# A second scalar for GpSimd's scaling of the attention weights where there is no gate

## The reference

```python
sk = sinks.astype(jnp.float32)[None, :, :, None, None]
m = jnp.maximum(jnp.max(s, axis=-1, keepdims=True), sk)
e = jnp.exp(s - m)
p = e / (jnp.sum(e, axis=-1, keepdims=True) + jnp.exp(sk - m))
```

## Time and profile before

| what | value |
|---|---|
| time, median of 3 runs | 2685.29 us (2681.62 to 2685.42) |
| the profiled execution | 2683.39 us, its span 2681.2 us |
| mean granted TensorE clock | 0.973 |
| PE busy | 2519.5 us (94%) |
| POOL busy | 1772.3 us (66%), 993 instructions |
| DVE busy | 1330.3 us (50%) |
| ACT busy | 715.8 us (27%) |
| swa attention | about 952 to 1032 us |
| na attention | about 1993 to 2094 us |
| ca attention | about 2145 to 2215 us |

### The profile page before, as it was taken

The page is one execution under the profiler, slowest core; times in us unless marked ns, Lnnn a source line. Parts: engine busy times, 40 slices in busy tenths (PEclk is TensorE's granted clock), DMA queues, the critical chain, the costliest instruction groups (busy, mean ns, idle before and its releaser), DMA issues. The chain is left out here.

```text
span 2681.2 us, 36597 instructions
## 1 busy us (share of the span) xinstructions
PE 2519.5 (94%) x11854; PEld 2038.9 (76%) x11854; DVE 1330.3 (50%) x2616; ACT 715.8 (27%) x1504; POOL 1772.3 (66%) x993
## 2 busy tenths in 40 slices
PE   8998889899999979899998999999999899999998
PEld 6786677588888767688886777777877777787877
DVE  6467886443342575411223566664138334751552
ACT  4305785301101263300112222222016232100002
POOL 4465455577777576577775544455779767687884
PEclk9998999999999989999999999999999999999999
DMA  7682001264563202233332311212423214233332
GB/s 262 188 232 72 1 1 39 94 206 153 176 194 94 63 17 91 74 98 94 96 100 71 102 56 57 62 56 66 108 83 71 82 50 123 79 105 91 89 104 75
DMA packets 420545, 259.73 MB, mean 97 GB/s; under 512 B 62844, under 2 KB 411513, under 8 KB 414017
## 3 DMA queue, kind: packets, MB, share of 16 engines
q1 hardware_dynamic: 395024, 199.47, 25.7%
q10 hardware_dynamic: 25393, 58.63, 6.6%
HBM read 253.86 MB, written 8.10 MB: 98 GB/s over the span
## 5 line engine op out<-in xcount | busy, mean ns | idle before, releaser
L677 POOL TENSOR_TENSOR W<-RAW,zeros 128x1024 fp32r<-128x1024 f32 (+2 forms) x349 | 668.2, 1915 | 657.8 <-PE PA L778 312.8
L684 POOL TENSOR_TENSOR W<-RAW,W 128x1024 fp32r<-128x1024 f32 (+2 forms) x355 | 849.1, 2392 | 49.2 <-ACT W L1543 19.4
L775 PE MATMUL PA<-H,W 128*128 128x512 f32 x1288 | 506.0, 393 | 7.7 <-DVEq L2412 2.3
L778 PE MATMUL PA<-H,W 128*128 128x512 f32 x1288 | 503.4, 391 | 0.0
L775 PE MATMUL PA<-A,W 128*128 128x512 f32 x944 | 373.9, 396 | 16.5 <-DVE A L2038 10.7
L778 PE MATMUL PA<-A,W 128*128 128x512 f32 x944 | 371.8, 394 | 0.0
L786 PE MATMUL PA<-H,W 128*128 128x512 f32 x1288 | 318.3, 389 | 0.0
L775 PEld LDWEIGHTS PA<-H,W 128*128 128x128 f32 x1288 | 242.3, 188 | 62.4 <-POOL W L677 7.4
L778 PEld LDWEIGHTS PA<-H,W 128*128 128x128 f32 x1288 | 242.4, 188 | 50.5 <-issue 0.5
L786 PEld LDWEIGHTS PA<-H,W 128*128 128x128 f32 x1288 | 241.7, 188 | 50.3
L786 PE MATMUL PA<-A,W 128*128 128x512 f32 x944 | 236.7, 393 | 0.0
(11 more groups left out here) (375 smaller groups left out, 3929.8 us busy)
## 6 DMA issues: line engine op xcount, KB each, us to landing
AD<-in_ada_w_dram ACTq DMA_DIRECT2D x40, 1024.0 KB, 5.1
RAW<-in_w_in_dram SPq DMA_DIRECT2D x160, 256.0 KB, 3.1
RAW<-in_mlp_w_up_dram SPq DMA_DIRECT2D x128, 256.0 KB, 3.0
RAW<-in_mlp_w_down_dram SPq DMA_DIRECT2D x128, 256.0 KB, 3.0
RAW<-in_w_up_dram SPq DMA_DIRECT2D x88, 256.0 KB, 3.1
RAW<-in_nsa_w_in_dram SPq DMA_DIRECT2D x40, 256.0 KB, 4.1
RAW<-in_w_down_dram SPq DMA_DIRECT2D x16, 384.0 KB, 3.4
RAW<-in_swa_w_in_dram SPq DMA_DIRECT2D x20, 256.0 KB, 3.3
```

Of the source, the lines that this page charges most:

```text
L677: e.tensor_tensor(W[0][:, s, 0:kc], RAW[:, s, 0:kc], zeros[:, 0:1].rearrange("p (a b) -> p a b", b=1).broadcast_to([P, kc, P]), ALU.add).t ...
L684: e.tensor_tensor(W[1][:, s, 0:kc], RAW[:, s, 0:kc], W[0][:, s, 0:kc].bitcast(F32), ALU.subtract).then_inc(w_split, 1)
L775: pe.matmul(PA[s][:, 0:n], W[0][:, s, k], hi, start=(k == 0), stop=False)
L778: mm = pe.matmul(PA[s][:, 0:n], W[0][:, s, k], lo, start=False, stop=False)
```

## The change

Where a unit has no gate, POOL's tensor_scalar gets a second scalar operand, the first column of the tile of ones, and a second multiplication. The product is the same number. L730 runs 112 times: 64 in swa, 32 in na, 16 in ca. No instruction is added, removed or moved, and no wait changes.

```diff
@@ -727,7 +727,7 @@
                 if grp["all"]:
                     pool.tensor_tensor(blocks4(w), blocks4(w), each4(inverse4, grp), ALU.mult).then_inc(sem("scaled"), 1)
                 elif grp["gate"] is None:
-                    pool.tensor_scalar(w, w, inverse, None, ALU.mult).then_inc(sem("scaled"), 1)
+                    pool.tensor_scalar(w, w, inverse, ones[:, 0:1], ALU.mult, ALU.mult).then_inc(sem("scaled"), 1)
                 else:
                     pool.tensor_scalar(w, w, inverse, grp["gate"][b], ALU.mult, ALU.mult).then_inc(sem("scaled"), 1)
```

## The result

The changed kernel takes 2691.8 us (median of 10 runs, 2685.72 to 2693.91), the kernel before 2684.26 us (median of 10, 2680.94 to 2687.55). The ratio is 1.0027, with a 95% interval from 1.0018 to 1.0037: slower by about 0.27%. The prediction was 2691.6 us. The profiled execution's span is 2689.6 us, 8.4 us above that of before.

The account below looks back on a forecast made before the run. It took na's ring through DVE and ACT, 11.97 us per head, as the bound: +7.9 us from blocking by L684, -1.6 at na's end, 0 in swa and ca, +6.3 on 2685.3 gives 2691.6 us; range 2679.5 to 2697.

Parts of the forecast that it names:

- Part 1: POOL's scalings without a gate: they take L732's 773 and 557 ns, some 70 us less of POOL's work.
- Parts 2 and 3: swa and ca: nothing waits for POOL's scaling there, so 0 us, bounds 0.5 us either way in each.
- Part 4: na: POOL's low split L684 starts earlier and blocks DVE's low queries and keys; +7.9 us over six heads.
- the ring: na: the cycle per head through DVE and ACT alone, from key parts to key parts; 11.97 us per head before.
- R: na: start of DVE's reciprocal of unit 4m+1; key parts foreseen done at R + 5.36, before at R + 3.69.
- PE has room, so it only idles longer: na: PE's own work is 11.1 of 13.4 us per head, so it only idles longer, some 2.2 us per head.
- rival (b): na: DVE is not blocked by L684, so the kernel gets faster; -5.1 us, 2680.2 us; chance 0.17.
- Part 5: na's last turn: PE waits for POOL's last scaling, which ends 2.0 us earlier; -1.6 us, bounds 0 and 2.0.
- its own range: Whole kernel, likeliest case: +4 to +8.5 us, from the parts' bounds and half a microsecond at each of six blockings.
- the within part: Whole kernel: chance that the time stays within 0.2%, 5.4 us, of no change; given as 0.15 + 0.14 + 0.08 = 0.37.
- Rival (a): na: PE's clock falls after the longer waits, on top of the blocking; +8.8 us in all, 2694.1 us; chance 0.17.
- Rival (c): L730 keeps its time, or blockings and gains cancel; 0, 2685.3 us, within 2 us; chance 0.15.

Follow-up runs that it names:

- e6_immediate: The change with the number 1.0 as second scalar instead of the column of ones; 2692.06 us, 1.0033 against the kernel before.
- e2_swa_ca_only: The kernel before with the second scalar in swa and ca alone, na left as before; 2686.30 us, 1.0003 against the kernel before.
- e4: The kernel before, one scalar everywhere, with na's low split moved behind the scaling of unit 4m+3; 2684.96 us, 1.0009 against the kernel before.
- e9: The change with na's low and rounded splits moved away from DVE's instructions with two SBUF inputs, placement faults mended; 2683.49 us, 0.9994 against the kernel before.

## Why the prediction was right

**Part 1, POOL's own time.** Right in kind, too high in size. L732's 773 and 557 ns became 823 and 723. The excess is waiting for the port. Of the wide ones a lone one takes 0.77 to 0.78, as the rows above show. Of the 64 narrow ones 43 stood beside no DVE instruction with two SBUF inputs and took 0.56, as L732 does; the other 21 took 1.06 on average. I foresaw 70 us less of POOL's work, the page has 55.4 less. The narrow ones fell short most: 64 x (1062 - 723) ns = 21.7 us instead of 32.3.

**Parts 2 and 3, swa and ca.** Right as far as can be told: -0.17 and +0.24 us, both inside the spread between profiles of one form, and the change in these two stages alone gives 1.0003, with an interval to 1.0012.

**Part 4, the ring.** The mechanism came out row by row: L684 at R + 1.00 (foreseen R + 1.0), the queries blocked and ending 0.55 us after it (0.55), the key parts done at 2019.24, R + 5.38 (R + 5.36), the bias add never at 2.34. By heads, the period against that of before:

| | foreseen | measured |
|---|---|---|
| first blocked head | +1.67 | 12.13 - 10.41 = +1.72 |
| second | +0.42 | 12.76 - 12.11 = +0.65 |
| four more | 4 x 1.45 = +5.8 | 54.28 - 47.76 = +6.5 |

Together +8.9 where +7.9 was foreseen; the mean period is 13.41 us (13.4). What missed is what the heads give back: it was put too high. In the second head the bias add gave back 2.34 - 1.31 = 1.03 us and not 1.25, for a scaling stood beside it (POOL at 2020.14 above); 1.67 - 1.03 = 0.64 is what was measured. In the four others I subtracted 0.22 us for shorter low values each time. But before the change they were longer in every other head only: 0.64 at 2052.19 and 0.65 at 2076.07, and 0.43 at 2040.40 and 0.42 at 2064.28. The row of 2040.40 stood in the earlier trace rows, and I read it as the price without the tail, not as a head of today. So two of the four heads had nothing to give back, and the others grew by 1.45 as foreseen (11.86 to 13.31). In the two that had nothing to give PE has become late besides: from the key parts to the reciprocal of unit 4m+1 they take 8.56 us instead of 8.33. DVE's timeline in one:

```profile
2053.23 0.69 DVE L1985 CUSTOM_DVE_ANT_0 sc<-PS,BIAS 128x512 f32<-128x512 f32 x1 [0.94 <-PE PS L998]
```

PE had started this head after 1.99 us of idle time, and DVE's mask now waits for its scores. "PE has room, so it only idles longer" failed at such places. The idle times themselves are shorter than the "over 2 us" foreseen: 1.77, 1.41, 1.99, 0.84, 1.98 and 1.02 us ahead of the six heads. e6_immediate shows the same two lengths of period, 13.22 and 13.61, at a granted clock of 1.00.

In one head DVE was first after all. DVE and POOL there (timeline, after):

```profile
2054.83 0.69 DVE L1962 TENSOR_TENSOR QS<-QN,QS 64x512 fp32r<-64x512 f32 x1
2055.55 3.49 DVE L1962 TENSOR_TENSOR KK1l<-KN,KK1h 64x512 fp32r<-64x512 f32 x2
...
2054.84 2.95 POOL L684 TENSOR_TENSOR W<-RAW,W 128x1024 fp32r<-128x1024 f32 x1
```

The queries, 0.01 us ahead, keep their 0.69 us; L684 takes 0.55 us longer than its 2.40, gets in between queries and keys, and the first key part takes the 2.8 us instead. That is what was said against rival (b): being second costs the same.

**Part 5, the end.** From the last key parts to the first panel of the projection: 22.3 us before, 20.2 after, -2.1 where -1.6 was foreseen (bounds 0 and 2.0, so a little outside). Part of it may not be the change's. In e2_swa_ca_only, where na is that of before, the same stretch took 21.5 us; against that it is -1.3. As foreseen, POOL's last scaling is no longer waited for, and the next late are ACT's copies and DVE's parts behind them: PE waits 0.84 us for `TURN` of L2010 at 2102.25.

**What was not in the sum.** The first period of na was 9.39 us in the profile of before and 10.4 to 10.6 in every other profile, e2's too. That microsecond belongs to the one execution profiled before, not to the change, and it is one of the clock: over the first 10 us from na's first scores the mean granted clock was 0.83 in that profile and 0.72 or 0.73 in the eleven others, those with one scalar in na among them. So +7.85 is 1.1 too high, and the sum of the ring and the end, 8.9 - 2.1 = +6.8, stands against +6.3 foreseen. Against e2_swa_ca_only, whose na is the same program as before's, it is 8.9 - 1.3 = +7.6. The measured +7.5 us of the medians is in its own range, +4 to +8.5, and 1.2 above the 6.3 foreseen. That the forecast of 2691.6 lies 0.2 us from the measured 2691.8 is luck: I added 6.3 to a median of before that came out 1.0 us lower (2684.26) when it was taken again from 10 runs.

The chances were added a hundredth off: the within part is 0.15 + 0.15 + 0.08 = 0.38, so 0.12 is left for faster. It changes nothing.

**Rival (a), the clock.** It fell, and cost next to nothing. Windows right after the new waits (columns as in rows 2), the change, then e6_immediate:

```profile
2019.20:2022.20 3.00, 2.92 (x17) 2.53 (x18) 2.93 (x7) 1.30 (x3) 0.77 (x1) 1.00 0.56 156
...
2045.30:2048.30 3.00, 2.95 (x10) 2.33 (x11) 2.91 (x7) 1.42 (x3) 0.77 (x1) 0.71 0.63 169
2048.30:2051.30 3.00, 3.00 (x17) 2.81 (x16) 2.29 (x6) 1.64 (x4) 1.52 (x2) 0.72 0.65 105
...
2072.30:2075.30 3.00, 2.89 (x11) 2.33 (x12) 2.90 (x8) 1.42 (x3) 0.77 (x1) 0.77 0.32 76
```

```profile
2042.40:2045.40 3.00, 2.94 (x17) 2.54 (x18) 2.91 (x8) 1.42 (x3) 0.70 (x1) 1.00 0.63 166
...
2069.20:2072.20 3.00, 2.90 (x17) 2.51 (x18) 2.91 (x8) 1.41 (x3) 0.70 (x1) 1.00 0.28 65
```

After the third and the fifth wait, the two longest (1.99 and 1.98 us), the mean granted clock was 0.71 and 0.77, so part of each window ran at 1.2 GHz, and of the one behind the first of them too; right after the others it was 1.00. In e6 it stayed at 1.00 after the same waits, and its periods there are 13.61 and 13.61 us where the change has 13.75 and 13.91. So two falls cost at most 0.45 us together, and e6 loses as much as the change (1.0033) without them. The 1.5 to 3.3 us of the rival were too much; that the ring's spare covered the falls fits this, but no run shows it by itself.

**Rival (c), by the rule that one and two operations cost alike** (the Trainium skill, GPSIMD Engine Reference, "Elementwise — side-by-side cycle accounting"): the trace doesn't agree. In na one operation took 1.56 us where no DVE instruction with two SBUF inputs stood beside it (e4, 2035.71) and two took 0.77, and e6 shows that it isn't the second operand's kind.

## What to carry to other kernels

A cheaper instruction on an engine with slack moves what stands behind it, so ask where the next one will land: here a 2.4 us split slid ahead of three DVE adds on which PE waits, and the kernel lost 7.5 us. Between GpSimd and VectorE what counts is who is where at the same time; a split placed where VectorE has no instruction with two SBUF inputs was worth 10.8 us of the stage against the same kernel with it in the wrong place. Before crediting busy time saved, look at how long the engine's own work is within the period of the ring: 30 us less of it in na were worth 3 of the stage at best, and less than can be told in the kernel's time.

## What the runs showed of the hardware

- A GpSimd tensor_scalar on 128x512 float32 takes 0.77 us with two operations and 1.56 with one. The dear one doesn't block longer: a key part beside it takes 1.07 us instead of 0.69 (before, at 2048.51), beside the cheap one 1.16 (after, at 2005.24).
- In the head of 2054.83 above, DVE was first by 0.01 us and kept the port, and a gap of 0.03 us between two DVE adds is enough for L684 to get in (POOL's row of 2054.84). Where two DVE adds overlapped, GpSimd did not get in between. In e9, POOL then DVE:

```profile
2055.01 2.00 POOL L730 TENSOR_SCALAR pr<-pr,stat_inv,cst 128x512 f32<-128x512 f32 x1
...
2054.96 0.41 DVE L1975 TENSOR_TENSOR VV<-VN,VV 128x256 fp32r<-128x256 f32 x1
2055.29 1.08 DVE L2395 TENSOR_TENSOR BIAS<-BIAS,cst 128x896 f32<-128x896 f32 x1
```

The values began 0.05 us before the scaling, and the bias add before they had ended; the scaling of 0.77 us took 2.00 and ended 0.64 us after the bias add. One head earlier the scaling was first (2042.94), and the values took 0.86 us. Such a toss of 0.05 us is one difference between e9's periods of 11.2 and 12.1 us; whether it is all of it is open, since the periods of before alternate too (11.86 and 12.02).
